# Hybrid decoder step: experts 0 and 1 in two parts, attention on nine query tiles from token 0

## The reference, cut to what matters

```python
def layer_norm(x, g, b): ...                       # over 1024 columns
xp = layer_norm(concat([meta, x_prompt]))          # 16 meta + 1024 prompt tokens
xs = layer_norm(x_sample)                          # 8 sequences x 8 tokens
q, k, v, logf, u, p = project(x, w_in, b_f)
att = fox(q, k, v, logf)                           # causal, 8 heads of 64, forget gates added to the scores
mix = concat([att, s5_mix(u), pool_mix(p)])
h = layer_norm(ALPHA * x + mix @ w_out, ln1_g, ln1_b)

def moe(h, w_router, b_router, w_gate, w_up, w_down):
    aff = sigmoid(h @ w_router)
    biased = aff + b_router                        # 16 experts in 4 groups
    gsel = argmax(sum of the two best of each group)
    _, idx = top_k(where(in_group(gsel), biased, NEG_INF), 2)
    w_sel = aff[idx] / sum(aff[idx])
    hid = silu(h @ w_gate[e]) * (h @ w_up[e]) * gates[e]
    return sum_e hid @ w_down[e]                   # 1024 -> 256 -> 1024

y = layer_norm(ALPHA * h + moe(h), ln2_g, ln2_b)   # the 16 meta tokens are dropped from y_prompt
```

## Time and profile before

| | us |
|---|---|
| median of 3 runs | 997.49 (997.23 to 998.46) |
| the profiled run | 994.33 |
| its span | 992.6 |
| PE busy in it | 912.7 (92%) |
| DVE, ACT, POOL busy | 423.7, 311.8, 212.7 |
| chain of waits: PE, DVE, ACT, DMA | 43%, 3%, 2%, 1% of the span |

### The profile page before, as it was taken

One profiled execution on the slowest core, in us unless ns is written; L12 is line 12 of the kernel. 1 busy time (PEld: TensorE's weight loads), 2 busy tenths in 40 slices (PEclk: granted clock), 3 DMA queues, 4 the chain that ended last, 5 costly groups with the idle time before them and its releaser, 6 DMA issues.

```text
span 992.6 us, 13623 instructions
## 1 busy us (share of the span) xinstructions
PE 912.7 (92%) x5025; PEld 579.4 (58%) x5025; DVE 423.7 (43%) x1244; ACT 311.8 (31%) x631; POOL 212.7 (21%) x289
## 2 busy tenths in 40 slices
PE   4999999999999999999899999994899999999785
PEld 4655645555566666666554444532788887878321
DVE  5689799612344343345424326648100001010156
ACT  6751505612233233225414233431212121211222
POOL 3089000011101346651021100432000000000155
PEclk9999999999999999999999999996999999999888
DMA  9540000465982025216441131457976888966293
GB/s 232 156 182 1 2 0 2 143 188 168 413 352 88 22 77 181 107 64 226 159 171 45 43 87 45 169 207 279 318 244 242 319 301 288 380 220 254 95 373 138
DMA packets 63677, 173.23 MB, mean 175 GB/s; under 512 B 17416, under 2 KB 26687, under 8 KB 58103
## 3 DMA queue, kind: packets, MB, share of 16 engines
q1 hardware_dynamic: 55047, 141.37, 41.0%
q0 software_dynamic: 8368, 30.41, 8.4%
q10 hardware_dynamic: 192, 0.52, 0.2%
HBM read 113.24 MB, written 59.11 MB: 174 GB/s over the span
## 4 chain that ended last, share of the span: by engine, by line
PE 43%; DVE 3%; ACT 2%; DMA 1%; issue 1%; ACTq 0%; POOL 0%; DVEq 0%
PE banks L2350 14%; PE banks L2185 11%; PE banks L2363 6%; PE banks L2465 2%; PE banks L2344 2%; PE banks L2376 1%; PE banks L2482 1%; PE banks L2296 1%; PE banks L2197 1%; PE banks L2269 1%; PE banks L2250 1%; PE banks L2217 1%; DVE xT L2744 0%; DMA x_slots<-xT,slot_i 0%; DVE arena L2814 0%
## 5 line engine op out<-in xcount | busy, mean ns | idle before, releaser
L1514 PE MATMUL banks<-xT,arena 128*128 128x384 f32 (+2 forms) x384 | 122.9, 475 | 5.7 <-DVE mx L1709 3.8
L2185 PE MATMUL banks<-arena,mixT 128*128 128x512 f32 x256 | 116.8, 602 | 0.0
L1514 PEld LDWEIGHTS banks<-xT,arena 128*128 128x128 f32 x384 | 71.4, 190 | 53.6 <-DVE mx L1709 10.5
L2185 PEld LDWEIGHTS banks<-arena,mixT 128*128 128x128 f32 x256 | 47.0, 193 | 49.5 <-issue 49.5
L2350 PEld LDWEIGHTS banks<-mixT,arena 128*128 128x128 f32 x512 | 70.4, 190 | 6.8 <-issue 6.8
L2350 PEld LDWEIGHTS banks<-mixT,v_tok 128*128 128x128 f32 x512 | 70.3, 190 | 4.3 <-issue 4.3
L2350 PE MATMUL banks<-mixT,arena 128*128 128x160 f32 x512 | 71.7, 300 | 0.8 <-ACT mixT L2564 0.8
L2350 PE MATMUL banks<-mixT,v_tok 128*128 128x160 f32 x512 | 70.9, 299 | 0.8 <-ACT mixT L2564 0.8
L2721 POOL DMA_INDIRECT arena<-y_park,slot_s x17 | 16.2, 951 | 250.6 <-DMA y_park<-arena 245.7
L1619 ACT ACTIVATE arena<-arena,mx 128x144 f32<-128x144 f32 (+7 forms) x64 | 50.2, 785 | 62.5 <-DVE mx L1709 62.1
L535 PE MATMUL banks<-mixT,xT 128*128 128x512 f32 x144 | 62.7, 594 | 0.0
(11 more groups left out here) (413 smaller groups left out, 1367.5 us busy)
## 6 DMA issues: line engine op xcount, KB each, us to landing
arena<-in_w_down SPq DMA_DIRECT2D x16, 1024.0 KB, 8.4
x_slots<-xT SPq DMA_DIRECT2D x4, 2048.0 KB, 15.4
y_park<-xT SPq DMA_DIRECT2D x4, 2048.0 KB, 32.5
v_tok<-in_w_gate SPq DMA_DIRECT2D x8, 1024.0 KB, 7.0
v_tok<-in_w_up SPq DMA_DIRECT2D x8, 1024.0 KB, 7.0
arena<-in_w_gate SPq DMA_DIRECT2D x8, 1024.0 KB, 6.4
arena<-in_w_up SPq DMA_DIRECT2D x8, 1024.0 KB, 8.6
arena<-x_slots SPq DMA_DIRECT2D x16, 512.0 KB, 5.3
```

What stands on the lines that cost most here:

```text
L1514: last = T.matmul(b[:, 0:cn], w[:, k, :], xT[:, k, c0:c0 + cn], start=(k == 0), stop=(k == KD - 1))
L2185: last = T.matmul(bank[half], mixT[:, k, META + t * P:META + (t + 1) * P], w_oh[half][:, k, :], start=(k == 0), stop=(k == KD - 1))
```

## The change

1. LN0: DVE does `centre(1)` before `dt_rows`, and `copy_high(0)` before `stats(2)`.
2. Attention: nine query tiles from token 0 instead of eight from token 16; the ninth has 16 rows and 1040 keys. The cell of 16 keys goes away in all others. A third group of inverses and outputs for the ninth tile; the weights of the next pair are both loaded by POOL at its first tile; the projection of the next pair is one tile later.
3. Routing: `BATCH = ((0, 4), (4, 6), (6, 7), (7, 9))`, other order on PE and DVE, `project(8)` in other banks and without the wait for the residual of tile 7. Before the last batch `prior` of experts 0 and 1 is raised to at least 128 places (`EARLY = 7`), so the tokens of tiles 7 and 8 have only rest places in these two experts. `NOV` becomes 15.
4. Experts 0 and 1: their 128 main rows are loaded once the scatters of tiles 0 to 6 have landed, and their gate and up run interleaved with the routing of tile 8. Their rest rows follow in `first_rests`, 64 matmuls of 256 columns on four groups of 32 columns of the array, and are put back by `turn_first_rests`. The loop begins at expert 2; the warm-up matmuls are gone. Expert 2 has weight buffers of its own; SP's order is rewritten.
5. Tail: the diagonal weights are made by ACT before the last silu, residuals 1, 3 and 0 are done ahead of the overflow block, the table for the square root is loaded ahead, the last tile is normalised by DVE alone. The overflow body uses banks 4 and 5 only, so its wait for the copies of the tile before stands at the start of a tile.

The core of the diff; `ranks` and `overflow_table` don't appear in it:

```diff
-NOV = 2 * TOKM // (CAP + 1)
+FIRST = 2
+NOV = FIRST + (2 * TOKM - FIRST * (REM + 1)) // (CAP + 1)
...
-            GROUPS = ((0, 4), (4, 8))
-            FILL = range(1, 7)
+            GROUPS = ((0, 4), (4, 8), (8, 9))
+            FILL = range(2, 8)
...
-                for t in range(NQ):
+                for t in range(NT):
...
                 def turn(i, t, bl):
+                    q = nq(t)
...
-                        for kb, k, q0, at in cells(t, bl):
-                            last = T.transpose(b[0:k, at:at + P - q0], sc[(NQ * i + t) % 2][h][q0:P, kb * P:kb * P + k],
-                                               ident[q0:P, q0:P])
+                        for j, kb in enumerate(bl):
+                            w = min(P, NPR - kb * P)
+                            last = T.transpose(b[0:w, j * q:(j + 1) * q], sc[(NT * i + t) % 2][h][0:q, kb * P:kb * P + w],
+                                               ident[0:q, 0:q])
...
-            BATCH = ((0, 4), (4, 6), (6, 8), (8, 9))
+            BATCH = ((0, 4), (4, 6), (6, 7), (7, 9))
+            EARLY = BATCH[2][1]
...
+                def first_rests():
+                    pe.wait_ge(s_hid, FIRST)
+                    for k in range(KD):
+                        for which in range(2):
+                            for e in range(FIRST):
+                                g = 2 * which + e
+                                last = T.matmul(bank[2][REM * g:REM * (g + 1), 0:DE], xall[:, e, k, MAIN:CAP],
+                                                (gate_w, up_w)[which](e)[:, k * DE:(k + 1) * DE],
+                                                start=(k == 0), stop=(k == KD - 1), tile_position=(0, REM * g))
+                    last.then_inc(s_fr, 1)
...
+                t = NT - 1
+                project(t, 0)
+                project(t, 1)
+                turn(t - 1)
+                project(t, 2)
+                route_parts(t - 1)
+                project(t, 3)
+                route(t - 1)
+                pe.wait_ge(s_xe[0], 16)
+                turn_rows(0, xe[0])
+                turn(t)
+                pe.wait_ge(s_gw[0], 16)
+                pe.wait_ge(s_xc, 2)
+                pe.wait_ge(s_res, NT)
+                gate_or_up(0, 0, js=(0,))
+                route_parts(t)
+                gate_or_up(0, 0, js=(1,), ks=range(0, 4))
+                route(t)
+                gate_or_up(0, 0, js=(1,), ks=range(4, KD)).then_inc(s_gt, 1)
+                pe.wait_ge(s_xe[1], 16)
+                turn_rows(1, xe[1])
+                pe.wait_ge(s_uw[0], 16)
+                gate_or_up(0, 1).then_inc(s_up, 1)
                 ranks(3)
-                for n in range(8):
-                    T.matmul(bank[n % 2], ident[:, :], mixT[:, 0, META:META + 512], start=True, stop=True)
...
+                gate_or_up(1, 0).then_inc(s_gt, 1)
...
+                down(0)
+                down(1)
                 pe.wait_ge(s_xr, 64)
...
+                first_rests()
...
+                residual(1)
...
+                residual(3)
...
+                residual(0)
...
+                overflow(pe, released, body, done)
+
+                residual(2)
...
+                    if t0 == EARLY:
+
+                        chain(V.scalar_tensor_tensor(prior[:, t0, 0:FIRST], cap16[:, 0:FIRST], float(MAIN),
+                                                     prior[:, t0, 0:FIRST], ALU.add, ALU.max))
```

More of the change, by code:

```diff
@@ L1553, in weigh @@
                         pe.wait_ge(s_out, n - 1)
-                    for kb, k, q0, at in cells(t, bl):
+                    at = (t % 4) * P if t < NT - 1 else 0
+                    for j, kb in enumerate(bl):
+                        w = min(P, NPR - kb * P)
                         for h in range(2):
[L1556 to L1560, removed]
+                            last = T.matmul(bank[6 + n % 2][HD * h:HD * h + HD, at:at + q],
+                                            v_tok[0:w, kb, i * P + h * HD:i * P + h * HD + HD],
+                                            pt[u % 2][h][0:w, j * q:(j + 1) * q],
+                                            start=(kb == 0), stop=(kb == min(t, NT - 1)))
+                    if bl[-1] == t:
                         last.then_inc(s_PV, 1)
@@ L1601, in _ @@
                     waiting = None
+                    inverses(i, 2)
             def copy_turned(eng, copy, h, i, t, bl, u, n):
+                q = nq(t)
                 eng.wait_ge(s_T[h], n)
-                w = sum(P - q0 for _kb, _k, q0, _at in cells(t, bl))
-                copy(pt[u % 2][h][:, 0:w], bank[4 + h][:, 0:w]).then_inc(s_cp[h], 1)
+                if t == NT - 1:
+                    copy(pt[u % 2][h][:, 0:(len(bl) - 1) * q], bank[4 + h][:, 0:(len(bl) - 1) * q])
+                    w = NPR - bl[-1] * P
+                    last = copy(pt[u % 2][h][0:w, (len(bl) - 1) * q:len(bl) * q],
+                                bank[4 + h][0:w, (len(bl) - 1) * q:len(bl) * q])
+                else:
+                    last = copy(pt[u % 2][h][:, 0:len(bl) * q], bank[4 + h][:, 0:len(bl) * q])
+                last.then_inc(s_cp[h], 1)
             @block.scalar
@@ L1640, in inverses @@
                         act.wait_ge(s_out, n)
-                    S.copy(inv, bank[4]).then_inc(s_cp[0], 1)
+                    w = sum(nq(t) for t in range(*GROUPS[grp]))
+                    S.copy(inv[:, 0:w], bank[4][:, 0:w]).then_inc(s_cp[0], 1)
                 def turned_block(i, t, bl, u):
@@ L2333, in body @@
                             for j in range(2):
-                                last = T.matmul(bank[6 + half], hid[5][:, j, 0:P],
+                                last = T.matmul(bank[4 + half], hid[5][:, j, 0:P],
                                                 w_dn[4][:, j * D + 512 * half:j * D + 512 * half + 512],
@@ new lines, in _ @@
+                weigh(3)
+                project(t, 2)
+                turn_outputs(3)
+                ranks(2)
+                project(t, 3)
+                t = NT - 1
+                project(t, 0)
+                project(t, 1)
+                turn(t - 1)
+                project(t, 2)
+                route_parts(t - 1)
+                project(t, 3)
+                route(t - 1)
+                pe.wait_ge(s_xe[0], 16)
+                turn_rows(0, xe[0])
+                turn(t)
+                pe.wait_ge(s_gw[0], 16)
@@ L2444, in _, with residual @@
                 down_rest(E // 4 - 1)
+                def residual(t):
+                    if t - 4 in SHIFT_DVE:
+                        pe.wait_ge(s_yv, shifted_no(t - 4))
+                    elif t >= 4:
+                        pe.wait_ge(s_gn2, t - 3)
+                    for half in range(2):
+                        cols = slice(512 * half, 512 * half + 512)
+                        T.matmul(duo[t % 4][:, cols], scaled_i, h_all[:, t, cols],
+                                 start=True, stop=False)
+                pe.wait_ge(s_al, 1)
+                residual(1)
+                pe.wait_ge(s_yA, out_no(E - 1))
+                pe.wait_ge(s_yD, out_no(E - 1))
+                residual(3)
+                pe.wait_ge(s_yA, out_no(E - 1) + 1)
+                pe.wait_ge(s_yD, out_no(E - 1) + 1)
+                residual(0)
                 pe.wait_ge(s_yA, out_no(E - 1) + 2)
```

537 lines of the change are left out of this document (322 added, 215 removed).

## The result

The changed kernel takes 1295.58 us (median; 1293.96 to 1314.29) against 997.36 before: a ratio of 1.300, 95% interval 1.297 to 1.302. The slowest run, 1314.29, is left out of the ratio. The prediction was 1302. The profiled execution took 1295.39 with a span of 1293.7.

The account below looks back on a forecast made before the run. It took TensorE, busy 92% of the span, as the bound. Span 992.6 - 0.5 + 2 - 20.0 - 3.2 - 5 = 965.9, plus 331 for two overflow passes and what lies round them, plus 4.9: 1302 us, range 1235 to 1385.

Parts of the forecast that it names:

- The count: Last routing batch: tile 8 summed over 128 rows, non-tokens lift experts 13 and 14 to 166 and 164, two flagged.
- A pass: Overflow body, once per flagged expert: nine tiles of 15.5, weight loads 11, start 1; 151.5 us, two passes 303.
- the handovers: Overflow body: seven handovers between engines in each tile, 0.9 us together, bounded by 0 and 0.35 each.
- The idle turns: Overflow block's inner loop: 13 turns not taken, each jumping the body, at 1.5 us each, 19.5 (0 to 52).
- The late routing: From late routing to expert 2: its gate begins at 707.6 instead of 727.63, -20.0 us (-12 to -24).
- The -3.2: Expert loop: one down of 3.44 us leaves the loop and one small turn comes in, -3.2 us.
- Attention: Attention part: -6.0 us for dropped small transposes and weighings, +6.5 for a ninth tile; +2 (-6 to +10).
- Tail: Kernel's end: residuals and table load leave the chain, last tile normalised on one engine, -5 us (-8 to -2).
- LN0: Start of the kernel: centre(1) goes ahead of a copy that waited for its DMA, -0.5 us (-1.6 to 0).
- The sum: Whole kernel: span 965.9 us without the overflow body, 331 for the body, 1296.9 of span, time 1302.
- the 4.9: Whole kernel: measured time taken as span + 4.9 us, from a span of 992.6 and a median of 997.49.
- Rival (a): Overflow body: no expert is counted over 160, the body is skipped as before, 971 us; chance 0.13.
- Rival (b): Overflow body: runs twice with PE at 1.2 GHz, matmuls double, 1515 us; chance 0.05 with other long cases.

Follow-up runs that it names:

- e1_count_tokens: The changed kernel with the last batch counted over 128 rows for tile 7 and 64 for tile 8: 969.92 us, ratio 0.973.
- e8_count_again: The kernel of e1_count_tokens, unchanged, run once more beside later kernels: 970.56 us, ratio 0.974.
- e11_interleaved: e1_count_tokens with tile 8's turn ahead of the wait for expert 0's rows, the last ranks in the middle of expert 0's up: 969.03 us, ratio 0.973.
- e4_two_turns: The changed kernel with NOV = 2, so the overflow block's inner loop has no idle turn: 1298.58 us, from 1282.77 to 1308.48.

## Why the prediction was right, point by point

- **The count.** Shown from both sides: undone, the body is gone and the time is 970; done alone in the kernel before, 1296. The step from an unchanged function (`rows = P if t0 < NQ else NSA`) and a changed table of batches to two flagged experts held. It needed the count of the tokens on the given inputs: by that count 159 and 157 of 160 places were taken, and 7 rows that aren't tokens were enough.
- **A pass.** The tile was put at 15.5 and is 15.36; its pieces were 0.89, 1.2, 7.5, 0.9, 3.44 and 0.69, and are 1.14, 1.08, 7.40, 0.82, 3.69 and 0.70; the handovers, put at 0.9 from no row, take 0.53. The loads, put at 11, took 10.4 and 13.1 from the first issue to the last landing. The first tile of each pass is 18.7 and 18.3 instead of 15.4, which the sum didn't have: its transposes run at a granted clock of 0.50 and its 64 matmuls at 0.73 and 0.77. From the first load's issue to the last down's end it is 307 us, put at 303.
- **The idle turns** were the worst term: 19.5 for 13, at 1.5 each; measured 0.60 each, 7.9. The row I took for it, 2.01 for the skipped block, stands ahead of a PE matmul and isn't a turn; I priced PE's jump over its body, but the turns on the path are POOL's. What the 2.01 consists of isn't shown. By the Trainium skill ("Advanced Engine Details and Errata", section Control Flow Timing) a turn of one branch and one compare-and-branch is an estimated 0.16 and 13 are 2; the measured 7.9 lies between, nearer to the page's. What shares the 0.6 isn't shown.
- **The wait at the start of a tile** was inside my 15.5 but not priced by itself: it is 1.09 a tile, an estimated 17 us of the 298.
- **The late routing** was put at -20.0 and -3.2 for experts; in the profiled execution of the changed kernel it is -15.5 at expert 2's gate, and -16.2 at the end of the experts, of which 1.0 had come before the mixer. With the count mended it is -21.4 and -21.7 in one profile (e1_count_tokens), of which 2.9 had come before the mixer, and -17.0 and -19.0 in another of the same kernel (e8_count_again), of which 0.5 had. The step at fault in the changed kernel's profile is expert 0's rows. I had let them be there in time, but the last scatter of tile 6 ran beside the weights and landed after 11.5, and PE stood 6.36 for the rows; down(1) ended at 705.8, put at 700.6. The last scatter of all landed late too, put at 695 and seen at 700.8, but PE waited only 0.62 for its rows, and e11_interleaved, with the last scatters 2.8 earlier, had expert 1's down only 1.1 earlier. The -3.2 came out as -0.7, -0.3 and -2.0; in the first two profiles PE waited 2.3 and 2.2 for later experts' rows, which I had called covered.
- **Attention** +2 forecast, none measured (interval of 5 us). **Tail** -5 forecast; -3.9 from the first gather on in the changed kernel, -5.8 in e1_count_tokens. **LN0** wasn't tried alone.
- **The sum** is nearer than its parts, and that is luck. Up to the end of the experts it had -21.7 and the profile has -16.2; from there to the first gather 331 more than before, and the profile has 321.2; behind that -5, and the profile has -3.9. These three miss by +5.5, -9.8 and +1.1 and leave -3.2 of span. Another -3.0 lies in the 4.9 by which I set the time above the span: it took the span of one execution and the median of others; within one execution the difference is 1.7.
- **Rival (a)** didn't come, and its 971 is about the time of the same change with the count mended (969.92 and 970.56). **Rival (b)**, a PE at half clock, came in part: see below.

## What to carry to other kernels

When a table of batches or tiles changes, look for the conditions that are decided by the first element of a batch: they sit in functions that the diff doesn't show. Rows that pad a tile were harmless in the ranks here and costly in the totals that feed a threshold; check how near the data is to the threshold. And a branch that never ran has a price all the same: its body's time times the chance that an edit makes it run.

## What the runs showed of the hardware that I had not expected

The same tile of the overflow body runs at two speeds. The 64 matmuls of line 2396 took 7.40 in 15 of 18 tiles of the changed kernel's profile, but 8.8 to 9.2 in 14 of 18 in the profile of e4_two_turns, the slowest of its four executions: in the first fourteen tiles, one after the other, while the last four took 7.40 again. Windows over one such tile of e4_two_turns (stretch; its length, then busy time of PE, PEld, DVE, ACT and POOL; granted clock, DMA share, GB/s):

```profile
990.46:993.00 2.54, 2.54 (x12) 2.54 (x13) 0.00 (x0) 0.00 (x0) 0.63 (x1) 0.52 0.94 368
993.00:996.00 3.00, 3.00 (x25) 3.00 (x25) 0.17 (x1) 0.00 (x0) 0.00 (x0) 0.84 0.09 31
996.00:999.50 3.50, 3.48 (x32) 3.28 (x30) 0.00 (x0) 0.00 (x0) 0.00 (x0) 1.00 0.00 0
```

and the beginning of the same step in a fast tile of the changed kernel:

```profile
952.84:956.50 3.66, 3.66 (x33) 3.66 (x34) 0.17 (x1) 0.00 (x0) 0.73 (x1) 1.00 0.72 287
```

In the slow tile the granted clock is 0.52, close to the 1.2 GHz level, at the start of the step, after eight transposes at 1.00 and a wait for ACT's copies, and it is back at 1.00, 2.4 GHz, before the step's end; the scatters run beside the step in both kernels, so they alone don't make the difference. The first tile of a pass, behind the wait for the weights, is slow in every profile with a body (8.79 to 10.13 for the 64 matmuls). A later slow tile is 16.99 instead of 15.36; e4_two_turns has twelve of these, an estimated 20 us, and the changed kernel's profile one. That is of the order of the spread of this kernel's times (1282.77 to 1308.48), but only one of its executions was traced, so that the spread comes from there isn't shown; nor is it for the changed kernel's highest, 1314.29, whose trace wasn't taken. What puts an execution into the one pattern or the other stays open. The Trainium skill, "TensorE: Matmul & The Clock Gate", section Loop structure matters more than you think, says that a copy out of PSUM doesn't break PE's warmth, in a loop where the next matmuls follow immediately. This tile loop, which my prediction counted as of that kind, isn't quite so: PE stands 1.25 at the copies and 0.83 at the start of a tile. So the page decides neither for the first pattern nor against the second.
